# Token sums of a feed-forward layer in scratch of their own, over its first two jobs, with other bank orders and transposes behind another wait

## The reference, cut to what matters

```python
def swiglu(x, w_up, w_down):
    gate, up = jnp.split(x @ w_up, 2, axis=-1)
    return (jax.nn.silu(gate) * up) @ w_down

    for i in range(DEPTH):
        ...
        x = x + y
        x = x + swiglu(rms_norm(x, norm_ffn[i]), ffn_w_up[i], ffn_w_down[i])
        gate = jax.nn.sigmoid(x @ ple_w_gate[i] + ple_b_gate[i])
        x = x + gate * (p[i] @ ple_w_proj[i])
```

## Time and profile before

| | before |
|---|---|
| median of 3 runs | 1919.31 us (1919.06 to 1920.29) |
| profiled execution, its own time | 1919.13 us |
| its span | 1917.4 us |
| TensorE matmuls busy | 1855.7 us (97%) |
| VectorE busy | 993.6 us (52%) |
| ScalarE busy | 770.3 us (40%) |
| POOL busy | 681.5 us (36%) |
| mean DMA rate | 110 GB/s |

### The profile page before, as it was taken

One profiled execution on the slowest core, in us unless ns is written; L12 is line 12 of the kernel. 1 busy time (PEld: TensorE's weight loads), 2 busy tenths in 40 slices (PEclk: granted clock), 3 DMA queues, 4 the chain that ended last, 5 costly groups with the idle time before them and its releaser, 6 DMA issues.

```text
span 1917.4 us, 33438 instructions
## 1 busy us (share of the span) xinstructions
PE 1855.7 (97%) x13458; PEld 1717.4 (90%) x13458; DVE 993.6 (52%) x1361; ACT 770.3 (40%) x1201; POOL 681.5 (36%) x582
## 2 busy tenths in 40 slices
PE   7999997999999999999999999999989999999997
PEld 7999997999999999998555655999988999999997
DVE  6777635633633632697766668222256426426313
ACT  4576734422332334543432343423444323323333
POOL 3333551342343344565120100544522422432541
PEclk9999999999999999999999999999998999999999
DMA  4222231323322322422488779332322322323221
GB/s 128 89 78 83 87 97 44 89 88 88 89 84 85 85 82 75 100 73 99 133 262 300 242 256 302 88 94 72 110 62 78 92 84 83 89 88 89 78 83 66
DMA packets 187307, 210.70 MB, mean 110 GB/s; under 512 B 24483, under 2 KB 150051, under 8 KB 187119
## 3 DMA queue, kind: packets, MB, share of 16 engines
q1 hardware_dynamic: 186946, 208.71, 35.5%
q10 hardware_dynamic: 224, 0.07, 0.0%
HBM read 168.09 MB, written 40.64 MB: 109 GB/s over the span
## 4 chain that ended last, share of the span: by engine, by line
PE 87%; DVE 5%; ACT 2%; issue 2%; DMA 2%; POOL 1%; SPq 0%; ACTq 0%; DVEq 0%; POOLq 0%
PE ps L2495 37%; PE ps L2637 24%; PE ps L2617 12%; PE ps L2976 2%; PE ps L2939 2%; PE ps L2878 2%; PE ps L2917 1%; PE ps L2812 1%; DMA out_ml_C_s_dram<-C_HALVES 1%; PE ps L2996 1%; POOL W_LO L750 1%; PE ps L2927 1%; DVE H_PAD L1836 1%; DVE B_LO L1939 1%; DVE GATE L1936 0%
## 5 line engine op out<-in xcount | busy, mean ns | idle before, releaser
L750 POOL TENSOR_TENSOR W_LO<-W_RAW,W_HI 128x512 fp32r<-128x512 f32 x384 | 528.0, 1387 | 618.3 <-ACT W_HI L1056 551.3
L1056 ACT ACTIVATE W_HI<-W_RAW 128x512 fp32r<-128x512 f32 x404 | 249.6, 628 | 501.6 <-PE ps L2495 248.4
L2495 PE MATMUL ps<-A_HI,W_HI 128*128 128x288 f32 x1016 | 222.3, 301 | 20.9 <-POOL W_LO L750 14.7
L2495 PE MATMUL ps<-A_LO,W_HI 128*128 128x288 f32 x1016 | 219.8, 298 | 0.0
L2495 PE MATMUL ps<-A_HI,W_LO 128*128 128x288 f32 x1016 | 219.8, 298 | 0.0
L2495 PEld LDWEIGHTS ps<-A_HI,W_HI 128*128 128x128 f32 x1016 | 165.6, 191 | 24.6 <-POOL W_LO L750 14.5
L2495 PEld LDWEIGHTS ps<-A_LO,W_HI 128*128 128x128 f32 x1016 | 166.0, 191 | 0.0
L2495 PEld LDWEIGHTS ps<-A_HI,W_LO 128*128 128x128 f32 x1016 | 166.0, 191 | 0.0
L853 POOL TENSOR_TENSOR G_LO<-GATED,G_HI 128x1152 fp32r<-128x1152 f32 x22 | 58.9, 2677 | 269.5 <-ACT G_HI L1286 269.5
L2637 PE MATMUL ps<-A_HI,W_HI 128*128 128x288 f32 x640 | 137.2, 296 | 0.0
L2637 PE MATMUL ps<-A_HI,W_LO 128*128 128x288 f32 x640 | 137.0, 296 | 0.0
(11 more groups left out here) (464 smaller groups left out, 4143.8 us busy)
## 6 DMA issues: line engine op xcount, KB each, us to landing
W_RAW<-in_ffn_w_up_dram SPq DMA_DIRECT2D x176, 256.0 KB, 2.9
C_HALVES<-in_state_mlstm_C_dram SPq DMA_DIRECT2D x64, 512.0 KB, 5.1
out_ml_C_s_dram<-C_HALVES SPq DMA_DIRECT2D x64, 512.0 KB, 5.4
W_RAW<-in_ffn_w_down_dram SPq DMA_DIRECT2D x88, 256.0 KB, 2.8
W_RAW<-in_ml_w_in_dram SPq DMA_DIRECT2D x64, 256.0 KB, 2.8
W_RAW<-in_rg_w_in_dram SPq DMA_DIRECT2D x48, 256.0 KB, 2.7
W_RAW<-in_ple_w_gate_dram SPq DMA_DIRECT2D x32, 256.0 KB, 2.8
W_RAW<-in_ml_w_out_dram SPq DMA_DIRECT2D x32, 256.0 KB, 2.9
```

The source lines that it names most:

```text
L750: pool.tensor_tensor(W_LO[:, s], W_RAW[:, s], W_HI[:, s].bitcast(F32), ALU.subtract).then_inc(lo_ready, 1)
L1056: act.activation(W_HI[:, s], W_RAW[:, s], ACT.Copy).then_inc(hi_ready, 1)
L2495: ins = pe.matmul(ps[:, 4 * s + 2 * m + h, 0:HALF_T], a[:, w, k, wc], x[:, h * HALF_T:h * HALF_T + HALF_T], start=i == 0 and k == 0 and q ...
```

## The change

Five things change, in both layers.

- `seven(g, j)` now leaves out the first two jobs of a layer: the second job becomes plain as well, and its weights need no sums.
- The token sums get tiles of their own: TOKEN_ROWS for the scaled rows and two TOKEN_SUMS in turn for the sums. They lie over tiles used at other times: the state output rows, and the weight sums, which are first needed in the third job.
- The order on ScalarE: each split goes first, pairs 0 and 1 are made in the first job (pair 1 behind SiLU), pairs 2 and 3 in the second. VectorE does `token_sums` 0 ahead of the first job's gate product and 1 behind it, 2 and 3 ahead of the second's. Since the tiles cover the state output rows, ScalarE's first `scaled_pair` of layer 1 waits for the eight stores; VectorE's wait for them goes.
- Banks: other starts, other down sets, and in the third group another order of the seven products over the first slab alone (FIRST_ORDER). The waits on banks are counted by turn, not by product.
- Ahead of `turn_in`, TensorE waits for the last gate combination alone (`combined`); the wait for the up banks (`up_out`) stands behind the transposes.

```diff
--- before.py
+++ after.py
@@ -47,7 +47,7 @@
 
 def seven(g, j):
 
-    return (g, j) != (0, 0)
+    return g > 0 or j > 1
 
 
 SEVEN_JOBS = [gj for gj in UP_JOBS if seven(*gj)]
@@ -60,8 +60,9 @@
 
 SUM_SLABS = {seven_first(layer, g, j) + k + 1 for layer in range(2) for g, j in SEVEN_JOBS for k in range(4)}
 LAYER_SUM_SLABS = 4 * len(SEVEN_JOBS)
-SEVEN_STARTS = [(0, 1, 2, 3, 4, 5, 6, 7), (0, 5, 6, 7, 4, 1, 2, 3), (0, 5, 6, 7, 4, 2, 3, 1)]
-DOWN_BANKS = [((0, 5, 6, 7), (1, 2, 3, 4)), ((0, 5, 6, 7), (1, 2, 3, 4)), ((0, 1, 2, 3), (4, 5, 6, 7))]
+SEVEN_STARTS = [(2, 0, 1, 3, 6, 4, 5, 7), (7, 0, 1, 6, 5, 2, 3, 4), (0, 4, 5, 6, 7, 1, 2, 3)]
+FIRST_ORDER = [(0, 1, 2, 3, 4, 5, 6), (0, 1, 2, 3, 4, 5, 6), (0, 3, 4, 5, 1, 2, 6)]
+DOWN_BANKS = [((0, 1, 6, 7), (2, 3, 4, 5)), ((0, 1, 6, 7), (2, 3, 4, 5))]
 
 
 def seven_number(layer, g, j):
@@ -72,7 +73,7 @@
 def seven_banks(g, j):
 
     a, b, c, d, e, f, k, x = SEVEN_STARTS[g]
-    for _ in range(j - (g == 0)):
+    for _ in range(j - (2 if g == 0 else 0)):
         a, b, c, d, e, f, k, x = d, f, k, e, x, b, c, a
     return (a, b, c, d, e, f, k), (tuple(sorted((x, a))), (b, c))
 HI_SLOTS, LO_SLOTS, RAW_SLOTS = (0, 1), (2, 3), (4, 5)
@@ -288,6 +289,10 @@
             SUM_LO = sb_in(p7, "SUM_LO", [P, 4, 3, P], F32R)
             above(p7, "norms7", 1)
             FIRST_PRODUCT = sb_in(p7, "FIRST_PRODUCT", [P, HALF_T])
+        with ExitStack() as pt:
+            above(pt, "weightst", 24 + 108 + 9 + 9)
+            TOKEN_SUMS = [sb_in(pt, f"TOKEN_SUMS{i}", [P, 2, T]) for i in range(2)]
+            TOKEN_ROWS = sb_in(pt, "TOKEN_ROWS", [P, 2, T])
         T_HI, T_LO = B_HI, B_LO
         with ExitStack() as p0:
             above(p0, "weights0", 24 + 36)
@@ -1246,13 +1251,13 @@
             def scaled_pair(i, gain):
 
                 for m in range(2):
-                    ins = act.activation(GATED[:, m, :], X[:, 2 * i + m, :], ACT.Copy, scale=VECS1[:, gain + 2 * i + m:gain + 2 * i + m + 1])
+                    ins = act.activation(TOKEN_ROWS[:, m, :], X[:, 2 * i + m, :], ACT.Copy, scale=VECS1[:, gain + 2 * i + m:gain + 2 * i + m + 1])
                 ins.then_inc(y_scaled, 1)
 
             def sums_hi(layer, i):
 
                 act.wait_ge(t_raw, 4 * layer + i + 1)
-                act.activation(T_HI[:, 2 * i:2 * i + 2, :], GATE[:, :, :], ACT.Copy).then_inc(t_hi, 1)
+                act.activation(T_HI[:, 2 * i:2 * i + 2, :], TOKEN_SUMS[i % 2][:, :, :], ACT.Copy).then_inc(t_hi, 1)
 
             def first_product(layer, g, j):
 
@@ -1264,13 +1269,25 @@
                 for g, (g0, gn) in enumerate(GROUPS):
                     for j in range(gn // 2):
                         for k in range(4):
-                            if not seven(g, j):
-                                scaled_pair(k, gain)
-                            elif k == 3:
-                                first_product(layer, g, j)
+                            if seven(g, j):
+                                if k == 3:
+                                    first_product(layer, g, j)
+                                split_hi()
+                                continue
+                            if (j, k) == (1, 0):
+                                scaled_pair(2, gain)
                             split_hi()
-                            if not seven(g, j):
-                                sums_hi(layer, k)
+                            if (j, k) == (0, 0):
+                                if layer:
+                                    act.wait_ge(stored, 16 * 8)
+                                scaled_pair(0, gain)
+                            elif (j, k) == (0, 1):
+                                sums_hi(layer, 0)
+                            elif (j, k) == (1, 0):
+                                sums_hi(layer, 2)
+                                scaled_pair(3, gain)
+                            elif (j, k) == (1, 1):
+                                sums_hi(layer, 3)
 
                         b = blk.adv()
                         if seven(g, j):
@@ -1281,6 +1298,10 @@
                         act.activation(GATE[:, :, :], GATE[:, :, :], ACT.Silu).then_inc(silu_done, 1)
                         for k in range(4):
                             split_hi()
+                            if (g, j, k) == (0, 0, 0):
+                                scaled_pair(1, gain)
+                            elif (g, j, k) == (0, 0, 1):
+                                sums_hi(layer, 1)
                         jobs.adv(8)
                         act.wait_ge(y_ready, b)
                         act.activation(gh[:, 2 * j:2 * j + 2, :], GATED[:, :, :], ACT.Copy).then_inc(y_hi, 1)
@@ -1931,12 +1952,13 @@
             def token_sums(layer, i):
 
                 dve.wait_ge(y_scaled, 4 * layer + i + 1)
-                x, t = pair4(GATED[:, :, :]), pair4(GATE[:, :, :])
+                raw = TOKEN_SUMS[i % 2][:, :, :]
+                x, t = pair4(TOKEN_ROWS[:, :, :]), pair4(raw)
                 link(dve.tensor_tensor(t[:, 0:4:2], x[:, 1:4:2], x[:, 0:2], ALU.subtract))
                 link(dve.tensor_tensor(t[:, 1], x[:, 3], t[:, 0], ALU.subtract))
                 dve.tensor_tensor(t[:, 3], x[:, 2], t[:, 1], ALU.subtract).then_inc(t_raw, 1)
                 dve.wait_ge(t_hi, 4 * layer + i + 1)
-                dve.tensor_tensor(T_LO[:, 2 * i:2 * i + 2, :], GATE[:, :, :], T_HI[:, 2 * i:2 * i + 2, :].bitcast(F32),
+                dve.tensor_tensor(T_LO[:, 2 * i:2 * i + 2, :], raw, T_HI[:, 2 * i:2 * i + 2, :].bitcast(F32),
                                   ALU.subtract).then_inc(t_ready, 1)
                 dve.wait_ge(t_ready, 4 * layer + i + 1)
 
@@ -2009,14 +2031,14 @@
                         if seven(g, j):
                             combine(layer, g, j)
                         else:
-                            for i in range(4):
+                            for i in ((2, 3) if j else (0,)):
                                 token_sums(layer, i)
                             dve.wait_ge(slab_used, jobs.adv(4) + 2 * RING)
                             dve.tensor_tensor(pair5(GATE[:, :, :]), psv[:, 0, :, :, 0:HALF_T], RB, ALU.mult).then_inc(psum_freed[0], 1)
                             uses[0].adv()
-                            if layer:
-                                dve.wait_ge(stored, 16 * 8)
-                        if j + 1 < ks:
+                            if not j:
+                                token_sums(layer, 1)
+                        if j + 1 < ks and seven(g, j + 1):
                             ahead(layer, g, j + 1, 0)
                         dve.wait_ge(slab_used, jobs.adv(4) + 2 * RING)
                         dve.wait_ge(silu_done, y)
@@ -2591,24 +2613,25 @@
 
                 q = seven_number(layer, g, j)
                 banks = seven_banks(g, j)[0]
-                first = j == (g == 0)
+                first = j == (2 if g == 0 else 0)
                 for i in range(4):
                     pe.wait_ge(lo_dve, dve_slabs.adv())
                     w = phase[0] % 4
                     phase[0] += 1
-                    for p, (weight, tokens) in enumerate(PRODUCTS):
+                    for turn, p in enumerate(FIRST_ORDER[g] if first and i == 0 else range(7)):
+                        weight, tokens = PRODUCTS[p]
                         if i == 0:
-                            if p == 0 and q % len(SEVEN_JOBS) == 0:
+                            if turn == 0 and q % len(SEVEN_JOBS) == 0:
                                 pe.wait_ge(t_ready, 4 * (layer + 1))
-                            if p == 0 and first:
+                            if turn == 0 and first:
                                 pe.wait_ge(psum_freed[0], uses[0].now())
-                            elif p == 0:
+                            elif turn == 0:
                                 pe.wait_ge(combined, 4 * q)
-                            elif p == 4 and first:
+                            elif turn == 4 and first:
                                 pe.wait_ge(psum_freed[1], uses[1].now())
-                            elif p == 4 or p == 5:
+                            elif turn == 4 or turn == 5:
                                 if not first:
-                                    pe.wait_ge(up_out, 2 * q - (p == 4))
+                                    pe.wait_ge(up_out, 2 * q - (turn == 4))
                         of_sums, at_k, at_m = FORMS[weight]
                         w_hi, w_lo = ((SUM_HI[:, w, at_k, :], SUM_LO[:, w, at_k, :]) if of_sums else
                                       (W_HI[:, w, at_k, at_m * P:at_m * P + P], W_LO[:, w, at_k, at_m * P:at_m * P + P]))
@@ -2680,13 +2703,13 @@
                             seven_job(layer, g, j, hi, lo)
                             up_job(layer, g, j, hi, lo)
                         else:
-                            job(0, 4, chunks(hi, lo), starts(acc, xn0))
+                            job(0, 4, chunks(hi, lo), None if j else starts(acc, xn0))
```

(2 more changed lines are left out.)

## The result

The changed kernel takes 1896.71 us (median of 4 runs, 1896.11 to 1898.99) against 1919.8 us before (4 runs, 1919.06 to 1920.29): ratio 0.9882, 95% interval 0.9865 to 0.9899. It is faster by 23.1 us. The forecast was 1889.9 us and a gain of 29.2, so the time lies 6.8 us above the forecast and the gain is 6.1 us short of it. The profiled execution took 1898.99 us (span 1897.3).

A forecast was written before the change was run, and what follows sets the result against it. TensorE's waits were taken as the bound, 36 us lost in both layers' windows; 1919.1 - 13.1 - 12.8 - 3.3 = 1889.9 us. Own range 1888 to 1892, wide range 1883.5 to 1897.

The forecast's parts named there:

- The window: First job's fourth gate slab to third job's gate half: 18.3 and 18.0 us lost; 52.7 us pure work after the change.
- Step 1: Second job of each layer becomes plain: 12 matmuls more, costing 1.65 us a layer.
- Step 2: New ScalarE, VectorE and POOL queues in the first jobs: window 56.3 us with 3.6 of gaps, gains 13.1 and 12.8.
- Rival A: VectorE isn't held by POOL in the window: 6.4 us more gain, 1883.5 us; chance 10%.
- Rival B: SiLU's table load holds ScalarE up to 2.80 us instead of 1.28: 1.1 us a layer, 1892.1 us; chance 15%.
- Rival C: Clock falls again at the third job's two close gaps: at most 5.1 us a layer, 1900 us; chance 12%.
- E: Slower: early small gaps lower the clock through the twelve plain slabs, up to 77 us in all, 1967 us; chance 1%.
- F: Stores hold ScalarE or sums stay tied to the gate tile, in layer 1 or both: 1904 to 1919 us; chance 4%.
- Step 3: ScalarE's wait in layer 1 for the eight stores: bounded by 0 and 25 us, taken as 0.
- Step 4: Per-layer transposes run ahead of the up-bank wait, hidden in VectorE's products: gain 3.3 us over both layers.
- D: G_LO at the down job or a bank start is late: up to 3.3 us of gain lost, 1893 us; chance 8%.
- Step 5: New bank order and pairs, same number of matmuls: cost 0; under 1.5 us at each of four group starts if late.

The follow-up runs named there:

- e10: The changed kernel with the second job's up product behind one pair of low parts and the third pair's rows scaled ahead of G_HI: 1888.86 us.
- e4: The changed kernel with the old order: all four pairs of token sums in the first job, scaled rows ahead of each split: 1916.42 us.
- e2: The kernel before with one edit, the wait for the up banks moved behind the per-layer transposes: 1915.33 us, ratio 0.9983.
- e8: The changed kernel with VectorE writing zeros instead of the low parts of the token sums, reading nothing: 1893.89 us (one run).
- e7: The changed kernel with e5's edit, and the second job's up product taken behind one pair of low parts instead of three: 1895.70 us.
- e9: The changed kernel with VectorE's up product of the second job behind one pair of low parts instead of three, a repeat run: 1896.58 us.
- e1: The changed kernel again, unaltered, against the kernel before: 1896.51 us, ratio 0.9888.
- e5: The changed kernel with ScalarE's splits of all four up slabs ahead of the sums' high part, in both plain jobs: 1898.21 us.
- e12: The kernel of e10 with the third up slab of the first job split ahead of the first pair's high part: 1891.10 us.

## Why the prediction was right, and where it was not

The direction and the mechanism held: the splits come in time, the clock stays up, the transposes hide. The size did not. 1896.71 us lies outside the forecast's own range of 1888 to 1892, and only just inside the wide one, whose upper end (1897) was kept for a clock that falls. It didn't fall, so that the time is inside the wide range is luck and nothing that the working earned.

**The window (its bound and pure work) was right.** 18 us a layer were lost in it, and they were to be had: the change took 10.5 and 10.3 of them, and e10 stands at 54.2 us against 52.7 of pure work.

**Step 1, the second job plain, 1.65 us a layer.** Not measured by itself. e4 doesn't speak against it: it has these matmuls without the better order, and its layers are 1.0 and 0.8 us longer than e2's.

**Step 2, the new queues: right in kind, wrong in size; this is the step that failed.** Forecast were gains of 13.1 and 12.8 us; they were 10.5 and 10.3. The term at fault is "POOL 1.30 a slab" together with "I let such a VectorE instruction wait". The forecast's own times for the third pair come out only if the second and the third subtraction wait for POOL; its first subtraction, the low part and the scaling wait for nobody, and POOL never waits for VectorE. In time from the root, ScalarE and VectorE ran to plan as far as the first job's up product (its end forecast at 326.8, which is 325.96 on the changed kernel's axis, where the root comes 0.84 us earlier; measured 325.94). Then the scaling L2058 took 2.09 us instead of 1.35, since POOL had two slabs in hand until 326.95. L1957 took 2.00 us instead of 0.79, behind G_LO. It held POOL's next slab in its turn (1.81 us instead of 1.30), and L1958 waited for that slab. The split that was forecast to end at 336.93, 336.09 on the new axis, ended at 337.77: 1.7 us late. In the first job POOL's pair took 3.18 us; in e8, where the pair takes 2.54, TensorE doesn't wait for it.

The forecast's gaps run from the time at which TensorE wants a slab to the time at which it starts. Taken in this way, the three gaps on POOL measured 0.70, 0.86 and 1.25 us, against 0.32, none and 0.50 forecast; the two of the third job were nearly as foreseen, 0.75 and 1.77 for 0.79 and 1.96. Together they are 5.3 us against 3.6, so 1.7 us more. A second term the forecast didn't have at all: behind each gap the first matmuls are spaced 0.11 us wider (0.5 in all), and the first pair of the window takes 0.48 us from start to start in place of 0.265. That makes 2.5 of the 2.6 us by which the window of layer 0 was short.

**Rival A (VectorE not held, 1883.5)** did not happen: there is more holding than forecast, not less. **Rival B (the table load holds ScalarE longer)** is refuted. The load started at 314.43 and SiLU at 316.19, 1.76 us later, and 0.03 us after the gate product's end (314.80 + 1.36 = 316.16); so no more than 1.76 us is the load's (1.70 in e8, where the gate product ends sooner behind the load's start). By the Trainium skill (ScalarE: Activation LUTs, What ACT_TABLE_LOAD costs) it would be 2.66 us with the drain, and by an estimate from that SiLU would start at 317.1. The 1.28 us of the load agree with it, the drain does not show. **Rival C (the clock)** did not happen in the change, 1.00 in both windows. The longest wait was 1.61 us there; e7 and e9 show a fall after waits of 1.82 and 2.75 us. **Rivals E and F** did not happen; e4, with the old order, has a time like F's worst case (1916.4 us).

**Step 3, the wait for the stores, 0.** Right: ScalarE's queue in layer 1 has the same waits as in layer 0, and the windows differ by 0.07 us.

**Step 4, the transposes, 3.3 us.** Right: e2 gives 3.3 by its ratio, with an interval of 1.3 to 5.0 us, and no wait for G_LO came in its place, so D did not happen either. **Step 5, banks, 0.** Nothing in the traces speaks against it: the only wait for banks among those listed is that of the third job's fifth product, which step 2 has. It was not tried by itself.

**The sum.** Against the forecast, the two windows miss 2.6 and 2.5 us. The other 1.7 us of the 6.8 lie outside the parts that the change touches. In e1, whose profiled execution (1896.41 us) is close to the median, 1.4 us are the mLSTM stage. It was 299.2 to 302.9 us long over the profiled executions, whatever the kernel, and 302.9 and 300.9 in the two of the changed kernel, against 299.5 before. Whether the change has a part in that is open; the kernel before has only one profile, and e10, with the same tiles, has 300.1.

## What to carry to other kernels

When work is spread over engines, write the queues out for VectorE and POOL together, not one after the other: if both instructions take all their inputs from SBUF, let whichever starts second do its work after the first one's end, in both directions. An order of instructions that has the pieces of VectorE's chain done before POOL's long instruction starts is worth more than making POOL's input earlier (e10 against e5 and e12). And an earlier split is not a gain in itself: ask whose work its follow-up will fall on. Where the same kernel's median moves by 3 us, compare the stretches that an edit touches, from start to start, before the medians.

## What the runs showed of the hardware that was not expected

- A VectorE instruction with two SBUF inputs holds POOL as well: two slabs 3.16 to 3.20 us beside a 1.36 us subtraction, 2.54 beside a memset (e8), 4.16 where three VectorE instructions fall on them (e10).
- SiLU can start 1.70 us after its table load has started (e8; 1.76 in the change; the load itself takes 1.28 us).
- A gap of TensorE costs 0.25 to 0.28 us beyond the idle time in its row (five gaps of the change, layer 0).
- After two waits of 1.43 and 1.82 us the clock stayed at its higher level in e5 and in e7's layer 1 and fell for about 3.5 us in e7's layer 0, with the same queues around them. Which of the two will happen couldn't be told from the rows.
